# Head sums and roots of a decoder trunk moved to fixed PSUM banks, with reordered dense units around the memory scores

## The reference, cut to what matters

```
def memory_kv(mem, p):                       # for the prompt's own memory
    kv = rms_norm(mem, p['ln_mem']) @ p['w_ckv']
    mk, mv = jnp.split(kv, 2, axis=-1)
    mk = rms_norm(mk.reshape(bsz, N_MEM, MEM_HEADS, MEM_HEAD_DIM), p['ck_norm'])
def memory_attend(h, mk, mv, p):
    q = rms_norm((h @ p['w_cq']).reshape(bsz, t, MEM_HEADS, MEM_HEAD_DIM), p['cq_norm'])
    s = jnp.einsum('bthd,bmhd->bhtm', q, mk) * (MEM_HEAD_DIM ** -0.5)
    pr = jax.nn.softmax(s, axis=-1)
    o = jnp.einsum('bhtm,bmhd->bthd', pr, mv)
```

## Time and profile before

| what | us |
|---|---|
| median of 3 runs | 1488.61 (1487.62 to 1494.21) |
| the profiled execution's own time | 1488.8 |
| its span, first to last instruction | 1487.0 |
| TensorE matmul busy | 1416.9 (95%) |
| VectorE busy | 947.4 (64%) |
| ScalarE busy | 597.1 (40%) |
| GpSimd busy | 124.3 (8%) |

### The profile page before, as it was taken

How to read it: one execution, slowest core, us unless ns; L and a number is a source line. 1 busy time by engine, 2 the same in 40 slices (tenths; PEclk the granted TensorE clock), 3 DMA queues, 4 the chain that set the end, 5 groups by cost and what they waited for, 6 DMA issues and landing times. The chain is left out here.

```text
span 1487.0 us, 28022 instructions
## 1 busy us (share of the span) xinstructions
PE 1416.9 (95%) x10902; PEld 1339.5 (90%) x10902; DVE 947.4 (64%) x1359; ACT 597.1 (40%) x854; POOL 124.3 (8%) x167
## 2 busy tenths in 40 slices
PE   5999999979999999999999999998799999999998
PEld 5999999858967799999999999998598778999998
DVE  5666656986655566665466664589766465666643
ACT  4333434444543343333343333442554433433332
POOL 3000000252010110000000000005310100000000
PEclk8999999999999999999999999999899999999999
DMA  8666445437467676654456654544465766556552
GB/s 260 170 169 169 157 159 166 157 130 252 151 231 251 236 184 169 169 168 157 139 163 166 169 169 157 174 152 142 140 236 170 247 242 219 150 163 168 162 172 94
DMA packets 298890, 263.95 MB, mean 178 GB/s; under 512 B 7287, under 2 KB 268917, under 8 KB 298775
## 3 DMA queue, kind: packets, MB, share of 16 engines
q1 hardware_dynamic: 279058, 203.28, 45.4%
q0 software_dynamic: 13776, 48.97, 9.3%
q10 hardware_dynamic: 5972, 10.54, 2.2%
HBM read 254.80 MB, written 8.56 MB: 177 GB/s over the span
## 5 line engine op out<-in xcount | busy, mean ns | idle before, releaser
L959 DVE TENSOR_TENSOR w_lo<-raw_weights,w_hi 128x1024 fp32r<-128x1024 f32 (+2 forms) x404 | 451.0, 1159 | 139.5 <-ACT w_hi L710 138.1
L1459 PE MATMUL pairs<-h_hi,w_hi 128*128 128x288 f32 x1760 | 522.9, 297 | 15.1 <-DVE h_lo L962 6.4
L1459 PE MATMUL pairs<-h_lo,w_hi 128*128 128x288 f32 x1760 | 523.7, 298 | 0.0
L1459 PE MATMUL pairs<-h_hi,w_lo 128*128 128x288 f32 x1760 | 521.5, 296 | 0.0
L710 ACT ACTIVATE w_hi<-raw_weights 128x1024 fp32r<-128x1024 f32 (+2 forms) x404 | 383.3, 999 | 280.6 <-PE pairs L1459 243.3
L1459 PEld LDWEIGHTS pairs<-h_hi,w_hi 128*128 128x128 f32 x1760 | 334.1, 190 | 19.1 <-issue 10.3
L1459 PEld LDWEIGHTS pairs<-h_lo,w_hi 128*128 128x128 f32 x1760 | 333.7, 190 | 0.6
L1459 PEld LDWEIGHTS pairs<-h_hi,w_lo 128*128 128x128 f32 x1760 | 333.3, 189 | 0.0
L1459 PE MATMUL pairs<-g_lo,w_hi 128*128 128x288 f32 x704 | 208.2, 296 | 0.0
L1459 PE MATMUL pairs<-g_hi,w_hi 128*128 128x288 f32 x704 | 208.1, 296 | 0.0
L1459 PE MATMUL pairs<-g_hi,w_lo 128*128 128x288 f32 x704 | 207.0, 294 | 0.0
(11 more groups left out here) (277 smaller groups left out, 1515.1 us busy)
## 6 DMA issues: line engine op xcount, KB each, us to landing
raw_weights<-in_w_ffn_in SPq DMA_DIRECT2D x176, 512.0 KB
raw_weights<-in_w_ffn_out SPq DMA_DIRECT2D x32, 1024.0 KB
raw_weights<-in_w_in SPq DMA_DIRECT2D x18, 1024.0 KB
mem_kv<-in_cache_mem_k POOLq DMA_DIRECT2D x16, 1024.0 KB, 5.4
raw_weights<-in_w_ckv SPq DMA_DIRECT2D x16, 1024.0 KB
raw_weights<-in_w_ffn_out SPq DMA_DIRECT2D x16, 768.0 KB
raw_weights<-in_w_out SPq DMA_DIRECT2D x8, 1024.0 KB
raw_weights<-in_w_cq SPq DMA_DIRECT2D x8, 1024.0 KB
```

Of the source, the lines that this page charges most:

```text
L959: return dve.tensor_tensor(out, in0, in1, op)
L1459: return pe.matmul(out, lhsT, rhs, start=start, stop=stop, **kw)
```

## The change

Three things change. First, the head sums of both stages and the spread roots no longer take turns: they go to fixed banks, with three semaphores of their own. Bank SCORES holds the sums, banks 0 and 1 hold the spread roots, and the second spread waits until VectorE has used the first. Second, the keys of samples 0 and 1 are copied by ScalarE alone, a whole pair at a time, and ScalarE frees the pair. Third, TensorE's order is different: the roots are spread after the keys of sample 0 and after those of sample 1, `ckv(1)` comes before `mem_scores(0)`, and `ckv(4)` before `mem_scores(7)`.

```diff
-    CX_ORDER += ["cq_stat"] + ["mem_k"] * 2 + ["cq_root"] * 2 + ["mem_k"] * 2 if _n == 0 else ["mem_k"] * 4
+    CX_ORDER += ["mem_k"] * 4
-MIX_ORDER = (["state_in"] + ["win"] * 2 + ["q"] * 2 + ["win", "qk_stat", "win", "att_k", "win", "att_k"] + ...
+MIX_ORDER = (["state_in"] + ["win"] * 2 + ["q"] * 2 + ["win", "win", "att_k", "win", "att_k"] + ...
...
 ScalarE, cross-attention
-                        act.activation(cq_rms[:, :], G[:, t % 2, 0, 0:T], ACT.Sqrt, ...).then_inc(rq_ready, 1)
+                        act.wait_ge(heads_summed, L * 2 + 2)
+                        act.activation(cq_rms[:, :], M[:, SCORES, 0:T], ACT.Sqrt, ...).then_inc(rq_ready, 1)
                     for b in (2 * n, 2 * n + 1):
                         for half in range(2):
+                            if b < 2:
+                                t = TURNS["mem_k"][2 * b + half]
+                                act.wait_ge(acc_ready, passed(L, 0, t))
+                                copy(mem_kt[:, b % 2, 4 * half:4 * half + 4, :]..., G[:, t % 2, :, :]...).then_inc(kt_half, 1)
+                                act.drain()
+                                act.wait_ge(acc_free, passed(L, 0, t - 1))
+                                act.sem_inc(acc_free, 1)
+                                continue
...
 VectorE, cross-attention
                         dve.wait_ge(rq_ready, L * 2 + 2)
-                        acc(L, TURNS["cq_stat"][0])
                         dve.reciprocal(cq_rms[:, :], cq_rms[:, :]).then_inc(r_ready, 1)
-                        free(dve.drain())
+                        for j in range(2):
+                            dve.wait_ge(cq_spread, L * 2 + j + 1)
+                            for e in range(2):
+                                for d in range(2):
+                                    k = 4 * j + 2 * e + d
+                                    last = stt(z[:, k, :], z[:, k, :], par(L, "cq_norm", d), M[:, e, 0:T], ALU.mult, ALU.mult)
+                            last.then_inc(cq_taken, 1)
+                        dve.drain()
+                        dve.sem_inc(z_done, 1)
+                        spread_q(dve, att=False)
+                    for b in (2 * n, 2 * n + 1) if n > 0 else ():
...
 TensorE, cross-attention
+                def spread_roots(j):
+                    if j == 0:
+                        pe.wait_ge(r_ready, L * 2 + 2)
+                    else:
+                        pe.wait_ge(cq_taken, L * 2 + 1)
+                    for e in range(2):
+                        hd = 2 * j + e
+                        ins = mm(M[:, e, 0:T], from_row(hd, 0), cq_rms[quadrant(hd), :])
+                    ins.then_inc(cq_spread, 1)
...
+                ckv(0)
+                pe.wait_ge(zsq_ready, L * 8 + 8)
+                for d in range(2):
+                    for hd in range(HEADS):
+                        ins = mm(M[quadrant(hd), SCORES, 0:T], into_row(0), squares[:, 2 * hd + d, :], d == 0, d == 1)
+                ins.then_inc(heads_summed, 1)
+                for b in range(2):
+                    mem_keys(b)
+                    spread_roots(b)
+                ckv(1)
+                pe.wait_ge(q_diag_ready, L * 3 + 3)
+                mem_scores(0)
+                for b in range(2, SAMPLES):
+                    mem_keys(b)
+                    mem_scores(b - 1)
+                    if b in (3, 5):
+                        ckv(b // 2 + 1)
+                ckv(4)
                 mem_scores(SAMPLES - 1)
-                ckv(4)
                 ckv(5)
```

More of the change, by code:

```diff
@@ L80 @@
 for _n in range(4):
-    CX_ORDER += ["cq_stat"] + ["mem_k"] * 2 + ["cq_root"] * 2 + ["mem_k"] * 2 if _n == 0 else ["mem_k"] * 4
+    CX_ORDER += ["mem_k"] * 4
 CX_ORDER += ["mkt", "mkt", "cx_s", "cx_s", "cx_pt", "cx_pt", "cx_o", "cx_o"]
-MIX_ORDER = (["state_in"] + ["win"] * 2 + ["q"] * 2 + ["win", "qk_stat", "win", "att_k", "win", "att_k"] + ["att_s"] * 2 + ["att_k"] * 4
+MIX_ORDER = (["state_in"] + ["win"] * 2 + ["q"] * 2 + ["win", "win", "att_k", "win", "att_k"] + ["att_s"] * 2 + ["att_k"] * 4
              + ["att_pt"] * 2 + ["att_k"] * 2 + ["tok"] * 3 + ["pool", "state_out"] + ["att_o"] * 2 + ["pw"])
@@ L309, in trunk_kernel @@
         mk_copied, ckv_taken = sem("mk_copied"), sem("ckv_taken")
+        heads_summed, cq_spread, cq_taken = sem("heads_summed"), sem("cq_spread"), sem("cq_taken")
         sp_passed, pool_passed, pe_passed = sem("sp_passed"), sem("pool_passed"), sem("pe_passed")
@@ L835, in _ @@
                     if n == 7:
-                        t = TURNS["qk_stat"][0]
-                        act.wait_ge(acc_ready, passed(L, 0, t))
-                        act.activation(qk_rms[0:64, :], G[0:64, t % 2, 0, 0:T], ACT.Sqrt, bias=small[0:64, 0:1], scale=1.0 / DH).then_inc(rq_ready, 1)
+                        act.wait_ge(heads_summed, L * 2 + 1)
+                        act.activation(qk_rms[0:64, :], M[0:64, SCORES, 0:T], ACT.Sqrt, bias=small[0:64, 0:1], scale=1.0 / DH).then_inc(rq_ready, 1)
                     if n == 8:
@@ L900, in _ @@
                     if n == 0:
-                        t = TURNS["cq_stat"][0]
-                        act.wait_ge(acc_ready, passed(L, 0, t))
-                        act.activation(cq_rms[:, :], G[:, t % 2, 0, 0:T], ACT.Sqrt, bias=eps, scale=1.0 / MDH).then_inc(rq_ready, 1)
+                        act.wait_ge(heads_summed, L * 2 + 2)
+                        act.activation(cq_rms[:, :], M[:, SCORES, 0:T], ACT.Sqrt, bias=eps, scale=1.0 / MDH).then_inc(rq_ready, 1)
                     for b in (2 * n, 2 * n + 1):
                         for half in range(2):
-                            if b >= 2 and half == 0:
+                            if b < 2:
+                                t = TURNS["mem_k"][2 * b + half]
+                                act.wait_ge(acc_ready, passed(L, 0, t))
+                                copy(mem_kt[:, b % 2, 4 * half:4 * half + 4, :].rearrange("p h c -> p (h c)"),
+                                     G[:, t % 2, :, :].rearrange("p e c -> p (e c)")).then_inc(kt_half, 1)
+                                act.drain()
+                                act.wait_ge(acc_free, passed(L, 0, t - 1))
+                                act.sem_inc(acc_free, 1)
+                                continue
+                            if half == 0:
                                 act.wait_ge(score_done, L * 16 + SAMPLES + b - 1)
@@ L1191, in _ @@
                 dve.wait_ge(rq_ready, L * 2 + 1)
-                acc(L, TURNS["qk_stat"][0])
                 dve.reciprocal(qk_rms[0:64, :], qk_rms[0:64, :]).then_inc(r_ready, 1)
-                free(dve.drain())
                 free(scaled(v_t[:, 0:2, :], win(7, 16, 18)[:, :, 0:T]))
@@ L1637, in _ @@
                 win(6)
-                pair = take(L, TURNS["qk_stat"][0])
                 pe.wait_ge(zsq_ready, L * 8 + 4)
@@ L1642, in _ @@
                     for g in range(2):
-                        ins = mm(pair[quadrant(g), 0, 0:T], cc("heads"), qk_squares[:, QUADS * g + j, :], j == 0, j == QUADS - 1)
-                ins.then_inc(acc_ready, 1)
+                        ins = mm(M[quadrant(g), SCORES, 0:T], cc("heads"), qk_squares[:, QUADS * g + j, :], j == 0, j == QUADS - 1)
+                ins.then_inc(heads_summed, 1)
                 win(7)
@@ L1845, in mem_values @@
                     ins.then_inc(v_used, 1)
-                pe.wait_ge(m_ready, L * 8 + 8)
[L1848 to L1872, removed]
```

## The result

| | before | after |
|---|---|---|
| median of 11 runs each, us | 1488.61 (1484.04 to 1494.21) | 1476.91 (1474.20 to 1481.62) |
| ratio after / before, 95% interval | | 0.9931 [0.9919, 0.9943] |
| profiled execution: its time, its span | 1488.8, 1487.0 | 1474.2, 1472.5 |

The kernel became faster by 11.7 us by the medians; 1477.0 was forecast. The ratio, which isn't the quotient of the two medians, says 10.3 us, with 8.5 to 12.1 as its interval, so that the medians meet the forecast to 0.1 us is luck. The same kernel was timed twice more in other jobs: 0.9918 [0.9897, 0.9939] and 0.9944 [0.9923, 0.9965].

A forecast was written before the change was run, and what follows sets the result against it. TensorE, 95% busy, was taken to bound the kernel. The start's 9.2 us and the end's 2.4, with copies and mixer at 0, sum to 11.6, giving 1477.0 us from 1488.61; 8 in 10 for 1474 to 1482.

The forecast's parts named there:

- What bounds the kernel: TensorE, busy 95% of the span: time is won only where it stands still or runs slowly.
- The start: Cross-attention, query heads' sums to `ckv(1)`: fixed banks and new order save 4.5 us in layer 0, 4.7 in layer 1.
- The walk: Step-by-step timing of layer 1's new start: 8.3 us from sums through `ckv(1)`'s start and `mem_scores(0)`, against 12.98.
- The cover: `ckv(1)` ahead of `mem_scores(0)` hides the second four multiplications and the laying out of queries, with 3.5 us of slack.
- ScalarE's copies: Whole-pair key copies of samples 0 and 1 by ScalarE, 1.02 us each: priced at 0, at worst 2 to 4 us lost.
- The end: `ckv(4)` ahead of the last scores removes a 1.39 us wait, less 0.2 charged: net 1.2 us per layer.
- The mixer: Head sums in the mixer lose their turn, where nothing waited: 0, at most 0.1 us gained.
- The clock falls in the new stretch too: Rival, 18%: granted clock falls between `ckv(0)` and `ckv(1)`, giving back 1.5 to 3 us per layer; 1479.5 to 1483.
- The end's wait only moves: Rival, 7%: `ckv(4)` or what follows inherits the 1.39 us and ScalarE's releases cost; 1481.5 to 1483.5 us.
- the fixed banks do nothing of use: Rival, 2%: the reciprocal, not the turn, sets `ckv(1)`'s time, leaving about the end's gain alone; 1486 us.
- The loads: Rival, 3%: loads of cached keys become the bound, TensorE waiting if one takes over 10.9 us; 1489 to 1492 us.
- More than the sum: Upper case, 5%: earlier arrival spares one of layer 1's low clock spells, another 3 us; 1473 to 1474.5.

The follow-up runs named there:

- e3: The changed kernel with `ckv(4)` back behind the last scores, `mem_scores(7)`; 1480.03 us, ratio 0.9954 to before.
- e1: The kernel before with only the mixer's head sums moved to bank SCORES, plus an empty turn to keep turns even; 1486.50 us, ratio 0.9994.
- e2: The changed kernel with `ckv(1)` back behind the first scores, `mem_scores(0)`; 1484.32 us, ratio 0.9974 to before.
- e8: The changed kernel with `ckv(1)` and `ckv(4)` back in their old places, so fixed banks and whole copies alone; 1489.12 us, ratio 1.0013.
- e4: The changed kernel with the keys of samples 0 and 1 copied in halves again by ScalarE and VectorE; 1477.05 us, ratio 0.9935.
- e7: The changed kernel with both samples' key transposes ahead of the first spread, and the second spread inside `ckv(1)`; 1479.45 us, ratio 0.9948.
- e9: The changed kernel with the mixer's convolution taps 16 to 20 one unit later on VectorE; 1478.57 us, ratio 0.9945.
- e6: The changed kernel with one more VectorE reciprocal of 288 columns ahead of the one that counts; 1483.95 us, ratio 0.9969.
- e5: The kernel before with only `ckv(1)` and `ckv(4)` moved ahead of their scores, turns and halves as they were; 1484.29 us, ratio 0.9984.
- the change again: The changed kernel, unedited, timed once more beside other runs on their chip; 1476.79 us, ratio 0.9918 to before.

## Why the prediction was right

**What bounds the kernel.** TensorE's idle and half-clock time in the two stages was the whole of what could be won there, and nearly all of it was: 54.98 us holds 0.71 us without work.

**The start, 4.5 and 4.7 us.** By e3 it is 4.50 and 4.78 us, or 4.41 and 4.50 against e1's stages. The walk slipped by tenths that cancel: `ckv(1)` starts 7.12 us after the sums in both layers (forecast 7.3), the wait for the reciprocal is 0.71 us (0.8), and the 0.1 us allowed ahead of the second spread did not come, although the multiplications take 1.79 us instead of 1.71, since the transposes beside them take 1.97. Of layer 1's 4.8 us, 2.84 - 0.71 = 2.1 is waiting that went, and (3.65 - 1.97) + (1.33 - 0.75) = 2.3 is the same work at the upper clock; the forecast had 1.7 of it. Its 2.84 us of idle time is layer 1's; in layer 0 the three waits of before are 1.64, 0.80 and 1.04 us, 3.48 together.

**The cover.** I gave `mem_scores(0)` a slack of 3.5 us under `ckv(1)`; it is 3.4 (1143.2 to 1146.59). The wait that stands there without it was expected at 2.4 us in e2, and e2 and e8 have 2.39. What the prediction did not say is how far the two parts depend on each other: in the stages either alone is worth about a quarter of the pair, and in the time neither is told from nothing.

**ScalarE's copies, priced at 0.** They take 1.02 us each as forecast. e4 shows 0.2 to 0.4 us per layer in their favour. For a reader of the Trainium skill: "PSUM — Partial Sum Buffer", section "Specifications (TRN2)", has both engines read different banks in parallel at full bandwidth, by which halves should free the pair sooner. In e4, as before, VectorE's half starts behind ScalarE's, and its cost is that VectorE's copies stand ahead of the multiplications, not that a pair comes free late. No run here has the halves side by side, so none shows what that would be worth.

**The end, 1.2 us.** The wait of 1.39 us is gone and 1.26 and 1.22 us came of it; the other 0.13 to 0.17 us I put down to the two more changes between dense and narrow products, charged at 0.2. `ckv(4)` found banks 2 and 3 free, and nothing that was named as late next came late: TensorE's only wait in each stage is the 0.71 us for the reciprocal, so none names `ckv_taken` or a load.

**The mixer, 0.** e1: 0.9994 [0.9974, 1.0015], and `win(7)` starts behind the sums without a wait as it did.

**The rivals.** *The clock falls in the new stretch too*: it did not in any of the change's six stages, nor in those of e3, e4, e7 and e9, fourteen in all. It was a real one all the same: with the wait of 2.39 us (e2, e8) it fell in 3 of 4 stages, with 2.74 us (e6) in 1 of 2. *The end's wait only moves* and *the fixed banks do nothing of use*: refused by e3, the second only because `ckv(1)` was moved as well. Without that e8 comes to 1489.12 us, but not for the rival's reason: TensorE's wait for the reciprocal is 0.71 us there too, and the 2.39 us for the queries are what takes the gain back. *The loads*: `mem_kv` lands in 5.3 / 5.5 / 8.4 us (5.2 / 5.5 / 8.4 before), under the 10.9 us of room. *More than the sum*: the medians don't show it.

The sum came out at 11.76 us in the stages against 11.6. By the three ratios the whole time fell by 10.3, 12.2 and 8.3 us. The last interval, 5.2 to 11.4 us, ends just short of 11.76, and the intervals of e7, e8 and e9 too end short of what their stages gained (11.6, 3.1 and 11.7 us). A microsecond or two may be given back outside the stages; where, no trace shows.

## What to carry to other kernels

A wait behind a small chain (sum, root, reciprocal, spread, multiply) is removed in two steps that are worth little alone: take the chain's intermediate results out of the buffers that the neighbouring work cycles through, and put a unit of independent work longer than what is left in front of its consumer. Price the idle time of TensorE together with the slower products that may run behind it. Before such an order is improved once more, look at what frees the next buffer: in e7 and e9 that wait stood right behind.

## What the runs showed of the hardware

**The clock follows the waits, not always.** In the six stages with the old start (before, e1, e5) TensorE waits 2.7 to 3.5 us in three pieces, and the granted clock fell to 0.50 in all six. In layer 1 of before and in layer 0 of e5 it fell behind the first piece already, of 1.63 us; in the other four it was 1.00 through the first two and fell with the third. These windows are layer 1 of before behind its first piece, then layer 0 in its third (the granted clock is the third number from the end):

```profile
1147.00:1148.00 1.00, 0.44 (x4) 0.00 (x0) 0.56 (x1) 0.34 (x1) 0.70 (x1) 0.60 0.00 0
1148.00:1149.00 1.00, 0.81 (x4) 0.51 (x4) 1.00 (x4) 0.00 (x0) 0.00 (x1) 0.50 0.64 86
...
415.00:416.00 1.00, 0.44 (x4) 0.00 (x0) 1.00 (x4) 0.00 (x0) 0.00 (x0) 1.00 0.69 66
```

With the wait of 0.71 us (0.42 in e7) and no longer one at the start it fell in none of fourteen stages. With one of 2.39 (e2, e8, behind 0.71) or 2.74 us (e6) it fell in four of six, in e8 in layer 0 and not in layer 1 of one execution. So waits of 1.63 us came with a fall in two stages and one of 2.74 us came without: the length of a wait alone doesn't decide, what does stays open, and such a wait has two prices, e6's 2.02 and 3.57 us.

**The rest of the program has two lengths.** Outside both stages the profiled executions take 1362.5 to 1366.5 us in nine traces, and 1369.8 to 1370.3 us in four: two of the change's three, e6 and e8. Most of the difference between after and the change again lies between the stages, in code that is the same. In the change again:

```profile
465.80:1011.20 545.40, 536.84 (x3997) 525.67 (x3997) 338.84 (x468) 212.01 (x284) 11.12 (x18) 0.99 0.56 170
```

It is 7.0 us longer than after's 538.42. Part of it is a weight load. ScalarE waited for it, then TensorE for the low part, and behind that TensorE ran at half clock until 559.4 (ScalarE's waits, TensorE's timeline, a window):

```profile
ACT w_hi L711 <- DMA raw_weights<-in_w_ffn_in: 4.7, 1, 4.7
```

```profile
553.49 0.61 PE L1463 MATMUL pairs<-h_hi,w_hi 128*128 128x288 f32 x1 [2.83 <-DVE w_lo L968]
```

```profile
553.00:557.00 4.00, 3.51 (x14) 3.51 (x15) 3.09 (x5) 1.58 (x4) 0.00 (x0) 0.50 0.22 65
```

In after the wait at this place is 1.36 us and the clock stays at 1.00. In the change again the products leave every 0.24 us instead of 0.13 from 553.9 to 559.4, which by my estimate costs 2.5 us, so that load and clock make some 4 of the 7 us. A second fall follows a wait of 2.51 us which after has too, at 745.04, without a fall:

```profile
749.73 0.37 PE L1463 MATMUL pairs<-h_hi,w_hi 128*128 128x288 f32 x1 [2.51 <-issue]
```

```profile
751.00:752.00 1.00, 1.00 (x6) 1.00 (x5) 0.43 (x1) 0.54 (x2) 0.00 (x0) 0.50 0.06 16
```

Such a wait for the low part is no mark of the four long traces alone. All four have it here (TensorE waits 2.1 to 3.2 us), with a fall of the clock behind it, and so have e9 (2.4 us, where no load is named) and before, with a load late by 4.1 us:

```profile
556.33 0.40 PE L1459 MATMUL pairs<-h_hi,w_hi 128*128 128x288 f32 x1 [2.22 <-DVE w_lo L959]
```

That is why one span against one span tells this change to 7 us only. The stage, start to start, came to 54.98 us in all six of the change's, where the clock held; where it falls, the same code differs by more (60.74 and 60.98 before, 60.65 and 60.70 in e1, 57.00 and 58.56 in e6). Whether the change makes a long execution more frequent (two of its three profiles, none of the three with the old start: before, e1, e5) stays open.
